# Turned input and spread norm roots in a fused GLA/SSD and mixture-of-experts block

## The reference

```python
def rmsnorm(x, w, eps=EPS):
    xf = x.astype(jnp.float32)
    y = xf * lax.rsqrt(jnp.mean(xf * xf, axis=-1, keepdims=True) + eps)
    return (y * w.astype(jnp.float32)).astype(x.dtype)

h = rmsnorm(x, norm_mix_w[l])
proj = h @ w_in[l]
```

## Time and profile before

| | us |
|---|---|
| median of 3 runs (3430.83 to 3432.09) | 3431.32 |
| profiled execution, its own time | 3430.52 |
| its span (first to last instruction) | 3428.9 |
| TensorE busy | 3353.7 |
| VectorE busy | 2183.7 |
| ScalarE busy | 1615.4 |
| GpSimd busy | 642.6 |

### The profile page before, as it was taken

One profiled execution on the slowest core, in us unless ns is written; L12 is line 12 of the kernel. 1 busy time (PEld: TensorE's weight loads), 2 busy tenths in 40 slices (PEclk: granted clock), 3 DMA queues, 4 the chain that ended last, 5 costly groups with the idle time before them and its releaser, 6 DMA issues.

```text
span 3428.9 us, 56739 instructions
## 1 busy us (share of the span) xinstructions
PE 3353.7 (98%) x21179; PEld 3048.5 (89%) x21179; DVE 2183.7 (64%) x2805; ACT 1615.4 (47%) x2091; POOL 642.6 (19%) x840
## 2 busy tenths in 40 slices
PE   7999999999999999999999999999999999999997
PEld 6778888888879999999999999988888888888986
DVE  5565556646556555555566666677767777777777
ACT  4444333333323444444444444555555555555555
POOL 1111111211133111111111211122122113212213
PEclk9999999999999999999999999999999999999998
DMA  9888898888847555555665666577677767867878
GB/s 382 349 341 311 308 333 299 311 330 300 308 182 223 169 173 175 179 177 177 184 192 180 202 199 196 165 239 230 197 222 229 240 213 223 248 215 234 255 239 311
DMA packets 475314, 826.58 MB, mean 241 GB/s; under 512 B 21853, under 2 KB 419325, under 8 KB 458816
## 3 DMA queue, kind: packets, MB, share of 16 engines
q1 hardware_dynamic: 443392, 721.84, 60.7%
q0 software_dynamic: 24320, 75.95, 9.5%
q10 hardware_dynamic: 7488, 27.27, 2.1%
HBM read 726.16 MB, written 98.96 MB: 241 GB/s over the span
## 4 chain that ended last, share of the span: by engine, by line
PE 87%; DVE 2%; DMA 2%; ACT 1%; issue 1%; POOL 0%; DVEq 0%; SPq 0%; POOLq 0%; ACTq 0%
PE acc L2527 13%; PE pp L2109 12%; PE acc L2523 11%; PE acc L2524 10%; PE acc L2525 10%; PE acc L2529 7%; PE acc L2539 4%; PE acc L2540 4%; PE acc L2541 4%; PE pp L2098 2%; PE tpm L2496 2%; PE tp L2075 1%; PE pp L2099 1%; PE tpm L2502 1%; DMA raw<-in_moe_w_down 1%
## 5 line engine op out<-in xcount | busy, mean ns | idle before, releaser
L1931 DVE TENSOR_TENSOR wlo<-raw,whi 128x2048 fp32r<-128x2048 f32 x384 | 876.0, 2289 | 306.6 <-ACT whi L1306 304.5
L1306 ACT ACTIVATE whi<-raw 128x2048 fp32r<-128x2048 f32 x384 | 730.1, 1910 | 156.7 <-PE acc L2541 103.0
L2527 PE MATMUL acc<-xhl,whi 128*128 128x512 f32 (+3 forms) x2304 | 763.8, 385 | 0.0
L706 POOL TENSOR_TENSOR gate_op<-gate_op 1x1 f32<-1x1 f32 x348 | 202.6, 582 | 2681.4 <-DMA xacc_d<-ybuf,tabb 522.9
L2529 PE MATMUL acc<-xhl,wlo 128*128 128x256 f32 (+3 forms) x2304 | 624.3, 271 | 0.0
L2523 PE MATMUL acc<-xhl,whi 128*128 128x272 f32 (+3 forms) x1792 | 534.9, 298 | 1.5 <-DVE xhl L1943 1.5
L2524 PE MATMUL acc<-xhl,whi 128*128 128x272 f32 (+3 forms) x1792 | 530.3, 296 | 0.0
L2525 PE MATMUL acc<-xhl,wlo 128*128 128x272 f32 (+3 forms) x1792 | 530.0, 296 | 0.0
L2527 PEld LDWEIGHTS acc<-xhl,whi 128*128 128x128 f32 x2304 | 432.0, 187 | 68.6
L1339 ACT ACTIVATE work<-acc,bgu 128x256 f32<-128x256 f32 (+7 forms) x400 | 173.3, 470 | 579.9 <-PE acc L2525 366.2
L2529 PEld LDWEIGHTS acc<-xhl,wlo 128*128 128x128 f32 x2304 | 437.3, 190 | 0.7
(11 more groups left out here) (357 smaller groups left out, 5340.1 us busy)
## 6 DMA issues: line engine op xcount, KB each, us to landing
u<-split_d SPq DMA_DIRECT2D x112, 2048.0 KB, 8.7
raw<-in_moe_w_gate SPq DMA_DIRECT2D x128, 1024.0 KB
raw<-in_moe_w_up SPq DMA_DIRECT2D x128, 1024.0 KB
raw<-in_moe_w_down SPq DMA_DIRECT2D x128, 1024.0 KB
split_d<-u SPq DMA_DIRECT2D x16, 2048.0 KB, 12.8
uraw<-in_w_in SPq DMA_DIRECT2D x12, 1024.0 KB, 11.1
yT<-in_moe_b_down SPq DMA_DIRECT2D x18, 512.0 KB
xin<-in_x ACTq DMA_DIRECT2D x14, 512.0 KB, 9.3
```

Source lines behind the costliest of these rows:

```text
L706: pool.tensor_tensor(gate_op[0:1, 0:1], gate_op[0:1, 1:2], gate_op[0:1, 1:2], ALU.add).then_inc(gate_ran, 1)
L1306: act.activation(whi[:, q % RING, :, :], raw[:, q % RING, :, :], ACT.Copy).then_inc(a_hi, 1)
L1931: dve.tensor_tensor(wlo[:, q % RING, :, :], raw[:, q % RING, :, :], whi[:, q % RING, :, :].bitcast(F32), ALU.subtract).then_inc(v_lo, 1)
L2527: pe.matmul(into[:, 0:2 * n].rearrange("p (c n) -> p c n", c=2), hi_, of[:, k, :, 0:n], start=(k == 0), stop=False)
```

## The change

The host passes x a second time, turned: `x_turned` of shape (8 pairs, 128, 8, 256), partition and block of the width before the token. In rounds s = 1 to 6, for tiles 4 to 15:

- ScalarE's queue reads the pair's turned x, 1 MB with 8 KB in a row for each partition, straight into `hraw`, at the top of the round, ahead of `sum_out`, once `h_lo(s)` has read `hraw`.
- `norm_sq` stays and so do `x_in` and the root; `norm_xn` goes. `x_in` waits for the squares of the tile before instead of for TensorE. GpSimd's root and ScalarE's squares get a wait each for the tile before.
- TensorE makes one transpose in place of eight: of the root column, stretched to 128 columns, which puts the 128 roots along the row of every partition, in `tp[:, 0:128]`.
- VectorE copies that to `roots_b` where `h_rows` was (step `dve_hT.root`, for which TensorE's later users of `tp` now wait), and multiplies the turned rows by weight and root later: for tile a + 2 ahead of the last x sum, for tile a + 3 ahead of `ssd_in(a, 0)`.

Rounds 0 and 7 compute as before. Two semaphores of the second stage become one.

```diff
+            roots_b = pa("roots_b", [P])
...
-            def norm_root(j, n):
+            def norm_root(j, n, turned=False):
                 after(pool, "act_norm.sq", j)
+                if turned:
+                    after(pool, "pe_tx.tx", j - 1)
                 own_wait(n)
...
             def x_in(j):
-                after(act, "pe_tx.tx", j - 2 if isinstance(j, int) and j == 2 else j - 1)
+                if isinstance(j, int) and j <= 4:
+                    after(act, "pe_tx.tx", j - 2 if j == 2 else j - 1)
+                else:
+                    after(act, "act_norm.sq", j - 1)
...
+                if tx and at >= 1:
+                    after(act, "dve_h.lo", s)
+                    act.dma_start(hraw[:, :, :], x_turned[bass.ds(s + 1, 1)].rearrange("one p k i -> (one p) k i")).then_inc(d_xt, 16)
                 if post:
                     after(act, "act_sqs.sqs", a - 2)
                     after(act, "dve_x2.a1", q)
...
-                if tx:
+                if tx and at == 0:
                     norm_xn(a + 3)
...
-                if more:
-                    norm_xn(a + 4)
...
+            def roots_out(j):
+                after(dve, "pe_tx.tx", j)
+                after(dve, "dve_hT.hT", j - 1)
+                done(dve.tensor_copy(roots_b[:, :], tp[:, 0:P]), "dve_hT.root")
+
+            def turned_rows(s, t):
+                after(dve, "dve_hT.root", s * 2 + 2 + t)
+                dve.wait_ge(d_xt, s * 16)
+                for k in range(KD):
+                    rows = hraw[:, k, t * P:(t + 1) * P]
+                    c = dve.scalar_tensor_tensor(out=rows, in0=rows, scalar=nw[:, k:k + 1], in1=roots_b[:, :],
+                                                 op0=ALU.mult, op1=ALU.mult)
                 done(c, "dve_hT.hT")
...
-                    h_rows(a + 2, 0)
+                    h_rows(a + 2, 0) if at == 0 else roots_out(a + 2)
...
                 if rec:
                     gla_add(b)
+                if tx and at >= 1:
+                    turned_rows(s, 0)
                 x_sum(s, 3)
...
-                    h_rows(a + 3, 1)
+                    h_rows(a + 3, 1) if at == 0 else roots_out(a + 3)
...
                     gate(q, 1)
+                if tx and at >= 1:
+                    turned_rows(s, 1)
...
                 ssd_in(a, 0)
...
+            def roots_spread():
+                done(pe.transpose(tp[:, 0:P], st[:, 1:2].to_broadcast([P, P]), ident[:, :]), "pe_tx.tx")
...
-                    after(pe, "act_norm.xn", a + 2)
+                    after(pe, "act_norm.xn" if at == 0 else "p_norm.rstd", a + 2)
...
-                    transposes(8, lambda c: xin[:, c * P:(c + 1) * P], "pe_tx.tx")
+                    if at == 0:
+                        transposes(8, lambda c: xin[:, c * P:(c + 1) * P], "pe_tx.tx")
+                    else:
+                        roots_spread()
...
-                        after(pe, "dve_hT.hT", a + 2)
+                        after(pe, "dve_hT.root", a + 2)
...
+    x_turned = _np.asarray(inputs["x"][0]).reshape(PAIRS, PW, KD, P).transpose(0, 3, 2, 1)
```

More of the change, by code:

```diff
@@ L81 @@
     "pe_tx": ["tx"],
[1 row of a table removed]
+    "dve_hT": ["root", "hT"],
     "act_h": ["hi"],
@@ L142, with build @@
 PRIMED = UNITS
-def build(nc, x, columns, shared, moe_cols, w_in, gla_w_alpha_up, w_out, router_w, moe_w_gate, moe_w_up, moe_w_down, moe_b_down, final_norm_w, out):
+def build(nc, x, x_turned, columns, shared, moe_cols, w_in, gla_w_alpha_up, w_out, router_w, moe_w_gate, moe_w_up, moe_w_down, moe_b_down, final_norm_w, out):
     with ExitStack() as ctx:
@@ L340, in done, with done_twice @@
             inst.then_inc(S[s], 1)
+        def done_twice(inst, first, second):
+            s, i = where[first]
+            assert turn[s] % len(STEPS[s]) == i and where[second] == (s, i + 1), (first, turn[s])
+            turn[s] += 2
+            inst.then_inc(S[s], 2)
         def after(eng, step, n):
@@ L353, in build @@
         d_un, d_st = ([sem(f"{n}{s}") for s in range(4)] for n in ("d_un", "d_st"))
-        d_x, d_x1 = sem("d_x"), sem("d_x1")
+        d_x, d_x1, d_xt = sem("d_x"), sem("d_x1"), sem("d_xt")
         d_xres, d_x2, d_h2 = ([sem(f"{n}{t}") for t in range(2)] for n in ("d_xres", "d_x2", "d_h2"))
@@ L370, in build @@
         d_bias = sem("d_bias")
-        v_cols, v_zero, v_one = sem("v_cols"), sem("v_zero"), sem("v_one")
+        v_cols, v_first = sem("v_cols"), sem("v_first")
         pe_u = sem("pe_u")
@@ L775, in body @@
                 if tx:
-                    norm_root(s * 2 + 3, n)
+                    norm_root(s * 2 + 3, n, at >= 1)
                     n = n + 1
@@ L787, in body @@
                 if more:
-                    norm_root(s * 2 + 4, n)
+                    norm_root(s * 2 + 4, n, True)
                     n = n + 1
@@ L987, in norm_sq @@
                 src = xres[:, 1, :] if second else xin[:, :]
-                done(act.activation(junk[:, :], src, ACT.Square, scale=1.0 / 32.0, accum_out=st[:, 0:1]), "act_norm.sq")
+                turned = not (isinstance(j, int) and j < 4)
+                if turned:
+                    after(act, "p_norm.rstd", j - 1)
+                c = act.activation(junk[:, :], src, ACT.Square, scale=1.0 / 32.0, accum_out=st[:, 0:1])
+                if turned:
+                    done_twice(c, "act_norm.sq", "act_norm.xn")
+                else:
+                    done(c, "act_norm.sq")
             def norm_xn(j):
@@ L1457, in h_rows @@
                                           heads(nw[:, 4 * b:4 * b + 4], 4, P), ALU.mult)
+                done_twice(c, "dve_hT.root", "dve_hT.hT")
+            def roots_out(j):
[9 more added lines that the diff above has]
+                                                 op0=ALU.mult, op1=ALU.mult)
                 done(c, "dve_hT.hT")
@@ L1924, in _ @@
                 dve.wait_ge(d_slots[t], 8 * TOPK * TILES)
-            dve.memset(fst[:, :], 0.0).then_inc(v_zero, 1)
-            dve.memset(yT[:, :, :], 0.0).then_inc(v_zero, 1)
+            dve.memset(fst[:, :], 0.0).then_inc(v_first, 1)
+            dve.memset(yT[:, :, :], 0.0).then_inc(v_first, 1)
             last = last_chunks(dve)
@@ L2011, in _ @@
             dve.wait_ge(d_vectors, 16)
-            dve.tensor_scalar(mcols[:, :, KD:2 * KD], mcols[:, :, KD:2 * KD], 1.0, None, ALU.add).then_inc(v_one, 1)
-            dve.wait_ge(v_one, 1)
+            dve.tensor_scalar(mcols[:, :, KD:2 * KD], mcols[:, :, KD:2 * KD], 1.0, None, ALU.add).then_inc(v_first, 1)
+            dve.wait_ge(v_first, 3)
             def scaled_rows(p):
@@ L2327, in body @@
                 if tx:
-                    after(pe, "act_norm.xn", a + 3)
+                    after(pe, "act_norm.xn" if at == 0 else "p_norm.rstd", a + 3)
                     if post:
@@ L2345, in body @@
                     if tx:
-                        after(pe, "dve_hT.hT", a + 3)
+                        after(pe, "dve_hT.root", a + 3)
                     else:
@@ L2514, in _ @@
             pe.wait_ge(v_xe[1], 1)
-            pe.wait_ge(v_zero, 2)
+            pe.wait_ge(v_first, 2)
             def products(q, n, b, ks, of):
@@ L2635, in _ @@
             chunk(i, SIZES[-1], True)
-_INS = ["x", "columns", "shared", "moe_cols", "w_in", "gla_w_alpha_up", "w_out", "router_w", "moe_w_gate",
+_INS = ["x", "x_turned", "columns", "shared", "moe_cols", "w_in", "gla_w_alpha_up", "w_out", "router_w", "moe_w_gate",
         "moe_w_up", "moe_w_down", "moe_b_down", "final_norm_w"]
@@ L2655 @@
     moe_cols = biases.reshape(E * 3 * KD, P).T
-    inputs = {**inputs, "columns": columns, "shared": shared, "moe_cols": moe_cols}
+    x_turned = _np.asarray(inputs["x"][0]).reshape(PAIRS, PW, KD, P).transpose(0, 3, 2, 1)
+    inputs = {**inputs, "x_turned": x_turned, "columns": columns, "shared": shared, "moe_cols": moe_cols}
     nc = _bacc.Bacc("TRN2", target_bir_lowering=False, num_devices=1)
```

## The result

The change takes 3462.3 us (3457.8 to 3464.1, 4 runs) against 3431.7 for the kernel before in the same comparison: ratio 1.0089, 95% interval 1.0077 to 1.0101. It is 30.6 us slower; 10 were forecast, and 3462 lies outside the range of 3421 to 3449. The profiled execution took 3463.1, its span is 3461.5 (before: 3428.9).

The account below looks back on a forecast made before the run. TensorE, 98% busy, was taken to bound the kernel. Stalls of 19.6 us, less 0.35 already there and 9.2 for transposes, gave +10.0 us on 3430.5: 3440.5, as a median 3441.3, said as 3441; range 3421 to 3449.

Parts of the forecast that it names:

- the chain: Second store's landing, ScalarE's scaling of sum 1, x block 1 copies, VectorE's addition, TensorE's third x block; reserves 0.05 to 2.53 us.
- five waits at x block 2: Sign expected in rounds 2 to 6: TensorE waits 3 to 5 us at the third of four x blocks.
- the transposes: TensorE, rounds 1 to 6: 84 transposes fewer at 0.109 us each, 9.2 us saved, all on the path.
- VectorE's cover: Eight added products, 2.3 us, fit VectorE's idle 4.77 us before the last x sum and 6.01 before the dt product.
- the step that decides: ScalarE's second store of the sums lands 4.5 us later behind the turned x, making TensorE wait at its third x block.
- the sum: Rounds 2 to 6: stalls 19.6 us, less 0.35 already there, less 9.2 for transposes: net +10.0 us.
- The delay of the store: Second store of the sums: 27 turns instead of 18 at 0.67 us each, free 4.5 us later.
- the bound: Worst case for the second store's delay: 9 turns at 1.0 us less 1.5 us of lead, 7.5 us; total 3456.
- One reserve: TensorE's slack at the third x block after its 0.76 us lead; one of five values was given as -1.11 us.
- gain alone: Rival: turned x passes in the 2.8 us hole before the weights' queue fills, stores hardly move; 3423 us, chance 0.22.
- Weights late: Rival: the added 1 MB delays weights at the end of six rounds, 2.2 us each; +4 us, 3435, chance 0.1.
- one piece for one piece: DMA engines alternate queues, a 16 KB weights piece for a 4 KB store piece; a turn takes 0.86 us.

Follow-up runs that it names:

- the filled run: Change with odd tile's scatter behind the root plus 30 idle transposes in rounds 2 to 6: 3443.8 us; 60 on the change unmoved: 3477.2 us.
- the earlier read: Changed kernel with the turned x issued some 18 us earlier, right behind the low part of h: 3430.9 us against 3436.9, ratio 0.9981.

## Why the prediction was wrong

The direction, the place and the chain were right: five waits at x block 2, in the rounds named, each behind the second store of the sums. So were the transposes (1.5 us a round in the run without the transfer; the stretched operand costs no more) and VectorE's cover (2.19 us in each place against 2.3 worked out). What failed is the size, in two terms of "the step that decides" and "the sum".

The delay of the store. The forecast took 4.5 us; it was 6.8 in the mean of the five rounds, and 8.4 in round 4 (18.3 against 9.9), outside even the 7.5 of the bound. So the waits are 30.5 us, where the sum had 19.6. The 4.5 were 27 turns at the mean of 0.67 us of the earlier trace rows, as if all parts of a store kept step. Half of the 16 closing words were indeed only 3.7 us later (13.6 against 9.9), but the last was 6.9 us later (18.9 against 12.0), and ScalarE waits for the last. One part of the excess has a cause that a run shows: once late, the store runs into GpSimd's scatter. With the scatter moved away the waits are 19.7 us. That this meets the 19.6 forecast is in part luck, since the single rounds differ from it by up to 2.3 us and round 6 did not gain. How small writes hold up the last part of a store is not shown. (One reserve is also off by 0.05: 385.04 - 385.34 - 0.76 is -1.06, which changes nothing.)

The clock. The sum had none: TensorE was taken to go on after a wait as before it. From the trace's times, (884.20 - 248.48) - (850.39 - 248.62) = 33.95 us more for rounds 2 to 6; waits +30.5 less 0.1, transposes -7.6, and some 11.1 are left, which the half-clock stretches behind the waits carry, as the filled run shows (10.3 there, by rounds). The whole: -9.2 + 30.4 + 11.1 = 32.3 us of the 32.6 by which the spans differ.

One reason given was also wrong in part. The forecast put the delay down to the turned x standing ahead in ScalarE's queue. Read on the sync queue it makes the store nearly as late (16.7 us against 18.3). In both cases the turned x fills the pause of the DMA engines at the turn of the round (share 0.83 and 1.07 instead of 0.52), which the rival "gain alone" assumed to be free for the taking. Put behind the stores it leaves the pause alone, and the long waits are gone. A filled pause alone does not decide it, as the earlier read shows: there one of 16 parts of the store was 8 us late in rounds 3 and 4 and none in 5 and 6. Why, stays open, and so does why the filled run stood still where it uses new weights. "Weights late" showed in no run of the change.

The Trainium skill (page "DMA: Bandwidth & Descriptors", Queues, rings and completion order) has a whole packet of typically 9 to 17 descriptors pass at a turn. The runs bear out the forecast's reading of one piece for one piece instead. With the weights' pieces halved, the waits fell from 30.5 to 1.2 us. And where the late part of the store can be followed alone, with the earlier read in round 3, its pieces start 0.77 us apart: one piece of 16 KB (0.61 us) and one of 4 KB (0.16).

## What to carry to other kernels

When an engine's list of waits is empty, its reserves are still worth a table: the landing of one store with 0.05 to 2.5 us of reserve cost 42 us (waits and half clock) when a transfer of 1 MB took a pause of the DMA engines that looked free. A store that someone waits for lands with its slowest part, so a mean of turns prices it too low; price it also by the traffic of the stretch into which it is delayed, small indirect writes included. A wait of several us on TensorE costs the half clock behind it too, here a third again. In this kernel it paid to put the new bulk transfer behind the short ones that someone waits for and to move the small scattered writes away from both.

## What the runs showed of the hardware

- Two hardware queues shared the DMA engines piece for piece where both had work: 112 packets each in 6 us at 1.84 and 0.39 MB. With 8 KB in place of 16 KB pieces the waits behind the 4 KB queue fell from 30.5 to 1.2 us.
- A store lands with the last of its 16 closing words: half of them at 13.6 us and the last at 18.9 in the change, and once (earlier read, round 3) fifteen by 11.6 us and the last at 19.2.
- Moving the scatter of 8-byte rows away from the store took 2.4 to 4.2 us off the waits of rounds 3 to 5, and 0.4 off that of round 6.
- After waits of 3.7 to 7.5 us TensorE's granted clock is 0.50 (1.2 GHz) for a while, 5.3 us behind the longest; with the waits cut to 0.3 to 2.2 us by idle transposes it stayed at 1.00 in rounds 2 to 6.
